# Subtracting a weight tile's low part on POOL in four instructions of 256 columns instead of one of 1024

## The reference

```python
proj = hn @ w_in                       # every layer
x = x + jnp.concatenate([mix, cross], axis=-1) @ w_o[i]
a = jax.nn.relu(h @ w_up);  x = x + (a * a) @ w_down
gu = h @ w_ffn_in[l];       x = x + (jax.nn.silu(g) * gu[..., D_FF_2:]) @ w_ffn_out[l]
```

## Time and profile before

| | |
|---|---|
| three executions | 2032.28, 2032.53, 2035.44 us |
| median | 2032.53 us |
| the profiled execution | 2034.07 us, span from first to last instruction 2032.3 us |
| granted TensorE clock, mean | 0.981 |
| PE matmul busy | 1958.4 us, 96% |
| DVE busy | 960.6 us, 47% |
| ACT busy | 771.6 us, 38% |
| POOL busy | 756.7 us, 37%, in 330 instructions |
| the 302 subtractions of L485 | 738.5 us, mean 2448 ns |

### The profile page before, as it was taken

How to read it: one execution, slowest core, us unless ns; L and a number is a source line. 1 busy time by engine, 2 the same in 40 slices (tenths; PEclk the granted TensorE clock), 3 DMA queues, 4 the chain that set the end, 5 groups by cost and what they waited for, 6 DMA issues and landing times.

```text
span 2032.3 us, 26265 instructions
## 1 busy us (share of the span) xinstructions
PE 1958.4 (96%) x9314; PEld 1596.9 (79%) x9314; DVE 960.6 (47%) x1848; ACT 771.6 (38%) x1379; POOL 756.7 (37%) x330
## 2 busy tenths in 40 slices
PE   6879999999999989999999997989999999999999
PEld 5756878888888878788888875668988888888887
DVE  5787723222224686332222258586732237666400
ACT  4445834232233477432232342324842233223221
POOL 3430034444444441344444433231024434444542
PEclk9989999999999999999999998988999999999999
DMA  5320022322232310222233232121022222232332
GB/s 199 104 73 22 1 83 83 104 94 93 94 95 91 100 41 22 94 94 93 96 97 97 93 100 73 52 63 42 1 63 94 94 94 93 94 102 93 104 104 73
DMA packets 46686, 167.67 MB, mean 83 GB/s; under 512 B 5312, under 2 KB 5632, under 8 KB 46336
## 3 DMA queue, kind: packets, MB, share of 16 engines
q1 hardware_dynamic: 45216, 162.55, 24.6%
q10 hardware_dynamic: 1376, 3.84, 0.5%
HBM read 164.28 MB, written 2.10 MB: 82 GB/s over the span
## 4 chain that ended last, share of the span: by engine, by line
PE 57%; DVE 3%; issue 2%; ACT 1%; DVEq 0%; ACTq 0%
PE bank L524 17%; PE bank L525 17%; PE bank L526 17%; PE bank L624 2%; PE bank L597 1%; PE bank L610 1%; PE bank L766 1%; ACT PROB L894 1%; PE bank L621 0%; PE bank L728 0%; DVE ACC L1176 0%; ACT XH L900 0%; ACT SQ L868 0%; PE bank L720 0%; PE bank L713 0%
## 5 line engine op out<-in xcount | busy, mean ns | idle before, releaser
L485 POOL TENSOR_TENSOR WL<-RAW,WH 128x1024 fp32r<-128x1024 f32 x302 | 738.5, 2448 | 1231.0 <-ACT WH L833 1231.0
L524 PE MATMUL bank<-XH,WH 128*128 128x512 f32 (+1 forms) x1480 | 595.3, 402 | 42.1 <-POOL WL L485 13.0
L525 PE MATMUL bank<-XL,WH 128*128 128x512 f32 (+1 forms) x1480 | 584.2, 395 | 0.0
L526 PE MATMUL bank<-XH,WL 128*128 128x512 f32 (+1 forms) x1480 | 583.4, 394 | 0.0
L833 ACT ACTIVATE WH<-RAW 128x1024 fp32r<-128x1024 f32 x302 | 317.1, 1051 | 351.0 <-PE bank L526 348.6
L524 PEld LDWEIGHTS bank<-XH,WH 128*128 128x128 f32 (+1 forms) x1480 | 281.1, 190 | 119.0 <-issue 27.9
L525 PEld LDWEIGHTS bank<-XL,WH 128*128 128x128 f32 (+1 forms) x1480 | 281.3, 190 | 62.8 <-issue 4.1
L526 PEld LDWEIGHTS bank<-XH,WL 128*128 128x128 f32 (+1 forms) x1480 | 281.0, 190 | 62.2
L526 PE MATMUL bank<-HH,WL 128*128 128x512 f32 x512 | 202.2, 395 | 0.0
L524 PE MATMUL bank<-HH,WH 128*128 128x512 f32 x512 | 202.2, 395 | 0.0
L525 PE MATMUL bank<-HL,WH 128*128 128x512 f32 x512 | 202.2, 395 | 0.0
(11 more groups left out here) (334 smaller groups left out, 2660.2 us busy)
## 6 DMA issues: line engine op xcount, KB each, us to landing
RAW<-stream SPq DMA_DIRECT2D x302, 512.0 KB, 3.7
X<-x SPq DMA_DIRECT2D x4, 512.0 KB, 7.6
out<-X SPq DMA_DIRECT2D x8, 256.0 KB, 4.4
MEM<-mem ACTq DMA_DIRECT2D x1, 1024.0 KB, 11.1
W<-cmp_w ACTq DMA_DIRECT2D x1, 1024.0 KB, 5.8
CT<-consts ACTq DMA_DIRECT2D x1, 656.0 KB, 13.4
POSB<-pos_rows ACTq DMA_DIRECT2D x2, 256.0 KB, 5.5
HR<-pos_rows ACTq DMA_DIRECT2D x1, 256.0 KB, 4.1
```

Source lines behind the costliest of these rows:

```text
L485: pool.tensor_tensor(WL[:, slot, :], RAW[:, slot, :], WH[:, slot, :].bitcast(F32), ALU.subtract).then_inc(lo_done, 1)
L524: pe.matmul(dst, lhs[0], rhs[0], start=start, stop=False)
L525: pe.matmul(dst, lhs[0], rhs[1], start=False, stop=False)
L526: return pe.matmul(dst, lhs[1], rhs[0], start=False, stop=stop)
```

## The change

POOL's subtraction is issued in four instructions of 256 columns each. The four run in order with no wait between them; the wait for ACT's high part stands ahead of the first as before, and only the fourth increments `lo_done`. Loads, high parts, matmuls and their orders are the same, and so are the waits of all other engines.

```diff
             def lo_part(n, slot):
                 pool.wait_ge(hi_done, n + 1)
-                pool.tensor_tensor(WL[:, slot, :], RAW[:, slot, :], WH[:, slot, :].bitcast(F32),
-                                   ALU.subtract).then_inc(lo_done, 1)
+                for piece in range(4):
+                    c = slice(piece * TW // 4, (piece + 1) * TW // 4)
+                    ins = pool.tensor_tensor(WL[:, slot, c], RAW[:, slot, c], WH[:, slot, c].bitcast(F32), ALU.subtract)
+                ins.then_inc(lo_done, 1)
```

## The result

The changed kernel takes 2012.97 us (median of six executions, 2011.57 to 2015.66), the kernel before 2031.88 in six; the ratio is 0.9906 with a 95% interval of 0.9894 to 0.9917, so 19 us or 0.94% faster. The forecast was 2030.5 with a range down to 2023.5: faster came true, at 0.32 of chance, but the size was ten times the forecast's 2 us and lies outside the range. The profiled execution took 2013.64 us, span 2011.7.

What follows compares the result with a forecast made beforehand. The prediction took PE's matmuls, 1958.4 of 2032.3 us, as the bound, with only its idle time to win. Its stretch terms summed to -1.9, rounded to -2.0 us, so 2032.53 becomes 2030.5 us; range 2023.5 to 2037.

Steps and rivals of the forecast that it cites:

- What bounds the kernel: Whole kernel: PE runs matmuls for 1958.4 of 2032.3 us; DVE delayed by POOL costs only at a few PE gaps.
- DVE and POOL exclude each other, POOL's pieces let DVE in: DVE instructions with two SBUF inputs wait out POOL's; between pieces DVE enters, a lone one waiting 0.7 us, not 2.2.
- What hides POOL: Outside the start, PE begins tiles long after POOL ends them; the last layer's tightest place has 5.6 us.
- The clock: Behind PE's gap at 29.45, a rival: granted clock may stay 1.00, giving 3.4 us back, 2027.1; chance 0.15.
- The price of a piece: POOL's subtraction of 256 columns: 0.82 us by a straight line; four in a row 3.2 us instead of 2.4.
- Pieces overlap: Rival on POOL's pieces: the fixed part hides behind the piece before, 0.60 to 0.75 us each; about 2024 us, chance 0.17.
- The replay: DVE and POOL replayed by instruction ahead of PE's gaps, ACT and PE times as observed; sum -1.9 us.
- to 1238.46: Last layer, 1219 to 1238: L1187 loses 0.9 instead of 3.3 us, L1553 0.6 instead of 2.1; in all -0.5 us.

Runs made afterwards that it cites:

- two-piece kernel: POOL's subtraction cut into two instructions of 512 columns a tile, against the kernel before with one of 1024: 2030.82 us, ratio 0.9988.
- put-off: Kernel before, subtractions whole; only the four that ran between 1219 and 1230 us wait until DVE is past its chain: 2032.15 us, ratio 0.9992.
- filled kernels: Kernel before, subtractions whole, plus matmuls with unread results in PE's gaps (12, 36 and 9 of them): 2035.12 us, ratio 1.0008.

## Why the prediction was wrong

The direction and the mechanism of the waits held. *What bounds the kernel* held: only the stages with PE gaps behind DVE moved, the long PE-bound ones by +0.2 and -0.1 us. *DVE and POOL exclude each other, POOL's pieces let DVE in* held: the longest QN, KML and K1L rows fell from 2.5 to 2.8 us to 0.86 to 1.12. *What hides POOL* held: waits for POOL stayed at two tiles. What failed is the sum. Three of its steps were wrong.

*The clock* was put at nothing in the sum. By PE's busy time it is the larger part of what was missed. I allowed for it at one gap, that of 29.45, and put 3.4 us on it, as a rival that excludes the others. PE's busy time fell by 12.3 us. The stretch at 0.50 behind 29.45 did go, with -3.7 us of busy time in the first stage, as that rival said. But the four gaps of the last layer's input stage each have such a stretch, its clock was 0.89, and I never priced it: 8.6 us of busy time went there. The granted clock of that stage could be read from the trace of the kernel before. And the two cases are not alternatives: the cheaper the piece, the shorter the gap and the higher the clock. Even so, my own prices for both, -7 and -3.4, give only 2022.

*The price of a piece* was too high. I drew the line from L504, a one-input operation of four columns, at 0.274 us (and rounded up: the line through both points gives 0.80, not 0.82). The subtraction's own fixed part is 0.18 us, a piece takes 0.737, and four in a row 2.82, not 3.2. The text had written down what that is worth: 0.75 us gave -7 us instead of -2. I gave this, the rival *Pieces overlap*, 0.17 and named a wrong mechanism for it; nothing overlaps more than I had assumed, the fixed part is only smaller.

*The replay, taken stretch by stretch,* was wrong in most places. The marks below are the same matmuls in both traces, by their times before, and the columns are how much earlier (-) or later PE comes through each stretch, in us:

| stretch | forecast | measured |
|---|---|---|
| start to the first sums, 29.45 | -0.7 | -2.0 |
| to 107.37 | +0.9 | -2.9 |
| to 122.02 | +0.4 | -0.6 |
| to the last layer's input stage, 1198.4 | 0 | +0.2 |
| to 1238.46 | -0.5 | -3.9 |
| to 1314.68 | 0 | -2.0 |
| to 1333.83 | -0.4 | -1.5 |
| to 1365.93 | -1.6 | -4.6 |
| to the end of that stage, 1392.9 | 0 | -3.2 |
| the rest | 0 | -0.1 |
| sum | -1.9 | -20.6 |

Two stretches have the wrong sign, and 5.2 us came in two stretches of the last layer that I had put at 0. At 1238 the text doesn't even follow from its own terms: they are 7.5 us lost before and 4.8 after, which is -2.7, and it put -0.5 without saying what the other 2.2 us are. The text gives no stretches for its -7 with pieces of 0.75 us, so how much of the miss is the price and how much the clock can't be told place by place. The two-piece kernel warns against reading them off PE's idle and busy time.

One reason lies in the method. The replay took what stands behind each gap from the observed times. The put-off and the filled kernels show what that misses: behind these gaps DVE has no slack, so whether a won microsecond is kept depends on whether DVE gets faster too. In this change it did, in the same stage, by 12.4 us of busy time (144.47 to 132.07), and both the waits and the clock stayed won here, while the same clock gained without a faster DVE was given back at once. This is shown for the gap at 1238 us and, with eight pieces, for the one at 107; for the gaps at 1333 and 1366 it is argued from them.

Of the observations that I had named, those at 102 us (8.57 against 9.34), 1366 (1.05, 1.5 shorter) and L1187's two (1.02) came as written. The first matmul (13.28, not 13.9) and the sums (27.45, not 28.7) came earlier. Missed were the bound of 1.5 us on DVE instructions with two SBUF inputs (L1555 takes 1.76) and that of 1.4 us on a piece beside DVE (the longest took 1.70). The gap at 1238 fell by 1.04, about the microsecond that I had given it, but this was no sign of a small gain. PE came to it earlier too: its waiting matmul stood 40.0 us behind the start of the stage before, and 36.1 after.

## What to carry to other kernels

Where a DVE instruction whose inputs all lie in SBUF runs several times its usual time, look for a POOL instruction beside it, and cut that one until a piece is short beside DVE's work, but stop before POOL's fixed cost eats its lead on its consumer; here eight pieces, with sixteen worse than four. Price a shortened PE gap together with the low-clock stretch behind it, from PE's busy time at the low clock in the whole stage, and ask of each gain whether the next engine in line can follow it.

## What the runs showed of the hardware that was not expected

- POOL's two-input subtraction costs 0.18 us plus 2.16 ns a column from 64 to 1024 columns (0.321, 0.461, 0.737, 1.292, 2.399 us). The fixed part is smaller than the 0.27 us of a one-input operation of four columns had led me to think.
- POOL and DVE take turns, also when POOL's instructions stand back to back with no wait between: eight KML of 0.42 us took 6.55 us beside pieces of 0.74. For a row of short DVE instructions four pieces are no gain (the sixteen KML take 0.81 us each on the mean after, 0.76 before), eight are (0.57); for lone and long ones four already are.
- A gap of 9.3 us, filled with unused matmuls, kept the granted clock at 1.00 (2.4 GHz) where it had been 0.50 (1.2 GHz) for 13.6 us. With whole subtractions it was worth nothing, with eight pieces 1.8 us at that place. Nine unused matmuls that ended 2.79 us ahead of the next one in use kept nothing: 17.1 us at 0.50 followed.
